# Picking experts on VectorE: masked copies over all heads at once, candidates' sums in two instructions, ranks in whole numbers

## The reference

```
v1, i1 = lax.top_k(s1, 16)          # (T, 8, 16); s2 likewise
v2, i2 = lax.top_k(s2, 16)
cand = (v1[..., :, None] + v2[..., None, :]).reshape(T, 8, 256)
sc, flat = lax.top_k(cand, 16)
e = take_along_axis(i1, flat // 16) * 128 + take_along_axis(i2, flat % 16)
g = softmax(sc)
out = sum over the 128 picks e of  g * gelu(x . u[e]) * v[e]
```

## Time and profile before

| | us |
|---|---|
| median of 3 runs | 1686.26 (1685.68 to 1686.49) |
| the profiled execution | 1687.21 |
| its span, first to last instruction | 1685.5 |
| TensorE busy in it | 1520.3 (90%) |
| VectorE busy | 1361.4 (81%) |
| GpSimd busy | 823.4 (49%) |
| ScalarE busy | 657.4 (39%) |
| mean granted TensorE clock | 0.951 of full |

### The profile page before, as it was taken

How to read it: one execution, slowest core, us unless ns; L and a number is a source line. 1 busy time by engine, 2 the same in 40 slices (tenths; PEclk the granted TensorE clock), 3 DMA queues, 4 the chain that set the end, 5 groups by cost and what they waited for, 6 DMA issues and landing times.

```text
span 1685.5 us, 25524 instructions
## 1 busy us (share of the span) xinstructions
PE 1520.3 (90%) x7943; PEld 1303.4 (77%) x7943; DVE 1361.4 (81%) x2701; ACT 657.4 (39%) x1101; POOL 823.4 (49%) x800
## 2 busy tenths in 40 slices
PE   4999799997978656768999999999999999999996
PEld 3677566684747545567999999999999999999995
DVE  5776544352579999848999999999999999999998
ACT  3332245421137663333443433434334334344343
POOL 1000100001029876637666676666666666766662
PEclk7999899998989857989999999999999999999998
DMA  9974121232000007899999999999999999999992
GB/s 348 357 267 159 64 73 50 100 129 74 1 1 1 1 13 227 256 299 407 406 403 385 382 382 388 383 379 392 383 379 387 388 379 384 386 383 384 384 387 103
DMA packets 193019, 448.90 MB, mean 266 GB/s; under 512 B 30699, under 2 KB 80131, under 8 KB 192716
## 3 DMA queue, kind: packets, MB, share of 16 engines
q1 hardware_dynamic: 136780, 243.65, 40.7%
q0 software_dynamic: 56192, 204.66, 31.0%
HBM read 424.57 MB, written 23.10 MB: 266 GB/s over the span
## 4 chain that ended last, share of the span: by engine, by line
PE 76%; DVE 12%; DMA 5%; issue 3%; POOL 2%; ACT 2%; SPq 1%; POOLq 0%; DVEq 0%; ACTq 0%
PE bank L818 13%; PE bank L993 9%; PE bank L992 9%; PE bank L991 9%; PE bank L1014 7%; PE bank L1012 7%; PE bank L1013 7%; PE bank L757 4%; PE bank L1004 3%; PE bank L1005 3%; PE bank L918 2%; DMA w_scratch<-staged 2%; DMA u_raw<-u_by_key 1%; DMA ring<-w_in 1%; POOL hot L692 1%
## 5 line engine op out<-in xcount | busy, mean ns | idle before, releaser
L991 PE MATMUL bank<-h_hi,u_hi 128*128 128x320 f32 x1024 | 316.5, 309 | 11.8 <-DVE u_lo L1807 11.8
L992 PE MATMUL bank<-h_lo,u_hi 128*128 128x320 f32 x1024 | 316.9, 310 | 0.0
L993 PE MATMUL bank<-h_hi,u_lo 128*128 128x320 f32 x1024 | 316.9, 309 | 0.0
L668 POOL DMA_INDIRECT v_rows<-v_exp,small x192 | 261.6, 1363 | 91.5 <-POOL small L664 51.8
L668 POOL DMA_INDIRECT u_rows<-u_exp,small x192 | 241.6, 1258 | 92.5 <-POOL small L664 51.2
L1323 ACT ACTIVATE v_hi<-v_raw 128x1024 fp32r<-128x1024 f32 x128 | 135.8, 1061 | 241.6 <-PE bank L1014 126.4
L991 PEld LDWEIGHTS bank<-h_hi,u_hi 128*128 128x128 f32 x1024 | 192.8, 188 | 17.2 <-issue 12.0
L1014 PE MATMUL bank<-v_hi,g_both 128*128 128x512 f32 x512 | 204.5, 399 | 0.0
L1012 PE MATMUL bank<-v_hi,g_both 128*128 128x512 f32 x512 | 203.6, 398 | 0.0
L1013 PE MATMUL bank<-v_lo,g_both 128*128 128x512 f32 x512 | 203.4, 397 | 0.0
L1807 DVE TENSOR_TENSOR u_lo<-u_raw,u_hi 128x1024 fp32r<-128x1024 f32 x128 | 157.4, 1231 | 55.2 <-ACT u_hi L1316 55.2
(11 more groups left out here) (247 smaller groups left out, 2940.4 us busy)
## 6 DMA issues: line engine op xcount, KB each, us to landing
u_raw<-u_by_key SPq DMA_DIRECT2D x128, 512.0 KB
v_raw<-v_exp SPq DMA_DIRECT2D x128, 512.0 KB
ada_blk<-ada_w SPq DMA_DIRECT2D x24, 1024.0 KB, 10.7
w_row<-w_scratch SPq DMA_DIRECT2D x128, 160.0 KB
ring<-w_in SPq DMA_DIRECT2D x18, 1024.0 KB, 5.1
w_scratch<-staged SPq DMA_DIRECT2D x2, 8192.0 KB, 30.8
xr<-x SPq DMA_DIRECT2D x8, 512.0 KB, 6.1
ring<-w_branch SPq DMA_DIRECT2D x4, 1024.0 KB, 5.1
```

What stands on the lines that cost most here:

```text
L668: pool.indirect_dma_start(out=rows[:, s], out_offset=None, in_=table, in_offset=bass.IndirectOffsetOnAxis(ap=ix[:, s:s + 1], axis=0))\
L991: pe.matmul(o, u_hi[:, r, k], h2_hi[:, k], start=(k == 0), stop=False)
L992: pe.matmul(o, u_hi[:, r, k], h2_lo[:, k], start=False, stop=False)
L993: last = pe.matmul(o, u_lo[:, r, k], h2_hi[:, k], start=False, stop=(k == KD - 1))
```

## The change

Four things change, all on VectorE:

- The masked copies of width 4, 2 and 1 run once over both halves of the heads instead of once per half. For that the lookup's scratch `halves` holds both halves; it lies in other places, one for tile 0, one for the tiles 1 and 2 (in two pieces 20 KB apart), one for tile 3. The piece of the tiles 1 and 2 takes the place of h2 of tile 1, so a wait for its transposes is added before pick(1).
- The sums of candidates are two instructions with four-dimensional patterns, all heads in each.
- The ranks stay whole numbers: the casts to float32 and back (L1689, L1704) go, and the instructions between read and write whole numbers.
- The two copies to `picks` stand together at the end.

```diff
--- before.py
+++ after.py
@@ -261,7 +261,15 @@
         top_i = at("top_i", 172, [P, 2 * PH, TOPK], U32)
         best = at("best", 173, [P, PH, TOPK])
         shifted = at("shifted", 173.5, [P, 2, P])
-        halves = at("halves", 28, [P, PH, TOPK, TOPK // 2])
+        halves_span = [at(f"halves{n}", kb, [P, kbs * 256]) for n, (kb, kbs) in enumerate(((35.5, 8), (167.5, 24), (135.5, 8)))]
+
+        def halves_of(t):
+
+
+            span = halves_span[(0, 1, 1, 2)[t]]
+            apart = 20 * 256 if t in (1, 2) else 1024
+            row = span.ap[0][0]
+            return bass.AP(span.tensor, 0, [[row, P], [apart, 2], [8, P], [1, 8]])
         starts = at("starts", 102.5, [P, P])
         expd = [at(f"expd{e}", kb, [P, P]) for e, kb in enumerate((91.5, 103, 108.5, 109))]
         h2 = [at(f"h2_{t}", kb, [P, D]) for t, kb in enumerate((183.5, 187.5, 183.5))] + [h2_own]
@@ -271,16 +279,14 @@
         def places_of(t):
 
             m = early if t == 0 else late
-            return (m[:, 0:384].bitcast(U32).rearrange("p (n h k) -> p n h k", n=3, h=PH),
-                    m[:, 384:768].rearrange("p (n h k) -> p n (h k)", n=3, h=PH),
-                    m[:, 768:1024].rearrange("p (h a k) -> p a h k", h=PH, a=2),
-                    m[:, 1024:1280].rearrange("p (n k) -> p n k", n=2 * PH))
+            return m[:, 0:384].bitcast(U32).rearrange("p (n h k) -> p n h k", n=3, h=PH), \
+                m[:, 1024:1280].rearrange("p (n k) -> p n k", n=2 * PH)
 
         def digits_of(t):
 
             m = early if t == 0 else late
             words = m[:, 0:1024].bitcast(U32).rearrange("p (n k) -> p n k", n=4)
-            return m[:, 768:1024], words[:, 0], (words[:, 1], words[:, 2], words[:, 3], words[:, 0])
+            return words[:, 3], (words[:, 1], words[:, 2], words[:, 0], words[:, 3])
 
         iota_f = small[:, 224:240]
         esum, einv = small[:, 240:248], small[:, 248:256]
@@ -1629,7 +1635,7 @@
 
                 stored(dve, *[("sc", t, q) for q in range(4)])
                 side = [scores[:, t % 2, n // 2, (n % 2) * NK:(n % 2 + 1) * NK] for n in range(2 * PH)]
-                place, place_n, pair, top_f = places_of(t)
+                place, top_f = places_of(t)
 
                 for n in range(2 * PH):
                     ins = dve.max(top[:, n, 0:8], side[n])
@@ -1646,12 +1652,12 @@
                 settled()
                 for i0, i1, nj in ((0, CORNER, TOPK), (CORNER, TOPK, CORNER)):
                     lo, n = (0, CORNER * TOPK) if i0 == 0 else (CORNER * TOPK, CANDS - CORNER * TOPK)
-                    shape = [P, i1 - i0, nj]
-                    for h in range(PH):
-                        ins = dve.tensor_tensor(
-                            cands[:, h, lo:lo + n].rearrange("p (i j) -> p i j", j=nj),
-                            top[:, 2 * h, i0:i1].unsqueeze(2).to_broadcast(shape),
-                            top[:, 2 * h + 1, 0:nj].unsqueeze(1).to_broadcast(shape), ALU.add)
+                    shape = [P, PH, i1 - i0, nj]
+                    by_side = top.rearrange("p (h a) k -> p h a k", a=2)
+                    ins = dve.tensor_tensor(
+                        cands[:, :, lo:lo + n].rearrange("p h (i j) -> p h i j", j=nj),
+                        by_side[:, :, 0, i0:i1].unsqueeze(3).to_broadcast(shape),
+                        by_side[:, :, 1, 0:nj].unsqueeze(2).to_broadcast(shape), ALU.add)
                 tick(ins)
                 for n in range(2 * PH):
                     ins = dve.max_index(top_i[:, n, 8:16], top[:, n, 8:16], side[n])
@@ -1686,49 +1692,43 @@
                     ins = dve.tensor_single_scalar(place[:, n], place[:, 0], by, ALU.logical_shift_right)
                 tick(ins)
                 settled()
-                tick(dve.tensor_copy(place_n, place))
-                settled()
-                i_of, j_of = pair[:, 0], pair[:, 1]
-                by_head = [place_n[:, n].rearrange("p (h k) -> p h k", h=PH) for n in range(3)]
+                as_number, ones_of = digits_of(t)
+                i_of, j_of = (as_number.rearrange("p (h a k) -> p h a k", h=PH, a=2)[:, :, a] for a in range(2))
                 first = starts.rearrange("p (h k) -> p h k", h=PH)
-                tick(dve.scalar_tensor_tensor(i_of, by_head[2], -float(TOPK - CORNER), by_head[1], ALU.add, ALU.max))
+                tick(dve.scalar_tensor_tensor(i_of, place[:, 2], -float(TOPK - CORNER), place[:, 1], ALU.add, ALU.max))
                 settled()
                 tick(dve.tensor_scalar(first, i_of, float(CORNER), float(CORNER * (TOPK - CORNER)),
                                        ALU.mult, ALU.add))
                 settled()
                 tick(dve.scalar_tensor_tensor(first, i_of, float(TOPK), first, ALU.mult, ALU.min))
                 settled()
-                tick(dve.tensor_tensor(j_of, by_head[0], first, ALU.subtract))
-                settled()
-                as_float, as_number, ones_of = digits_of(t)
-                tick(dve.tensor_copy(as_number, as_float))
+                tick(dve.tensor_tensor(j_of, place[:, 0], first, ALU.subtract))
                 settled()
                 for n in range(4):
                     tick(dve.tensor_scalar(ones_of[n], as_number, 3 - n, 1, ALU.logical_shift_right, ALU.bitwise_and))
                 settled()
 
 
+                wide, halves = [P, PH, TOPK, TOPK // 2], halves_of(t)
                 for half in range(2):
-                    sides, rows = slice(PH * half, PH * half + PH), slice(4 * TOPK * half, 4 * TOPK * half + 4 * TOPK)
-                    wide = [P, PH, TOPK, TOPK // 2]
-
-                    def where(n, width):
-                        at_half = ones_of[n][:, 2 * 4 * TOPK * half:2 * 4 * TOPK * (half + 1)]
-                        return at_half.rearrange("p (n k) -> p n k", n=PH).unsqueeze(3)\
-                            .to_broadcast([P, PH, TOPK, width])
-
-                    tick(dve.tensor_copy(halves, top_f[:, sides, 0:TOPK // 2].unsqueeze(2).to_broadcast(wide)))
+                    sides = slice(PH * half, PH * half + PH)
+                    at_half = ones_of[0][:, 2 * 4 * TOPK * half:2 * 4 * TOPK * (half + 1)]
+                    to = halves[:, half].rearrange("p (n k) j -> p n k j", n=PH)
+                    tick(dve.tensor_copy(to, top_f[:, sides, 0:TOPK // 2].unsqueeze(2).to_broadcast(wide)))
                     settled()
-                    tick(dve.copy_predicated(halves, where(0, TOPK // 2),
+                    tick(dve.copy_predicated(to, at_half.rearrange("p (n k) -> p n k", n=PH).unsqueeze(3).to_broadcast(wide),
                                              top_f[:, sides, TOPK // 2:TOPK].unsqueeze(2).to_broadcast(wide)))
+                settled()
+                for n, width in ((1, 4), (2, 2), (3, 1)):
+                    where = ones_of[n].rearrange("p (a k) -> p a k", a=2).unsqueeze(3).to_broadcast([P, 2, P, width])
+                    tick(dve.copy_predicated(halves[:, :, :, 0:width], where, halves[:, :, :, width:2 * width]))
                     settled()
-                    for n, width in ((1, 4), (2, 2), (3, 1)):
-                        tick(dve.copy_predicated(halves[:, :, :, 0:width], where(n, width),
-                                                 halves[:, :, :, width:2 * width]))
-                        settled()
-                    tick(dve.tensor_copy(picks[t][:, 0:2, rows].rearrange("p a (h k) -> p a h k", h=4),
-                                         halves[:, :, :, 0].rearrange("p (h a) k -> p a h k", a=2)))
-                    settled()
+                for half in range(2):
+                    rows = slice(4 * TOPK * half, 4 * TOPK * half + 4 * TOPK)
+                    ins = dve.tensor_copy(picks[t][:, 0:2, rows].rearrange("p a (h k) -> p a h k", h=4),
+                                          halves[:, half, :, 0].rearrange("p (h a k) -> p a h k", h=4, a=2))
+                tick(ins)
+                settled()
 
 
             def divide(t):
@@ -1756,6 +1756,7 @@
             multiplied(dve, ("h2T", 0, 0), ("h2T", 0, 1))
             h2_step(2)
             h2_step(3)
+            multiplied(dve, ("h2T", 1, 0), ("h2T", 1, 1))
             pick(1)
             pick(2)
             divide(1)
```

## The result

The changed kernel took 1688.47 us (median of 15 runs, 1686.61 to 1691.16), the kernel before 1686.17 (15 runs, 1684.08 to 1687.5): a ratio of 1.0017, with an interval of 1.0009 to 1.0024. It is 2.3 us slower. I had forecast 1684.9, and 1681.3 to 1687.2. The profiled execution took 1689.51 us with a span of 1687.8, 2.3 more than before.

A forecast was written before the change was run, and what follows sets the result against it. VectorE's picks were taken to bound the start of L1769, with GpSimd's line 5.2 us behind as cover. VectorE saves 7.5, GpSimd loses 3.8: 5.2 - 3.8 = 1.4 us gained, 1684.9 us; range 1681.3 to 1687.2.

The forecast's parts named there:

- What bounds the kernel: Before L1769 (`h_lo`): VectorE's picks end last; GpSimd's hot rows, staging and `h_hi` are late by 5.2 us less.
- Sums: Sums of candidates (L1651) on VectorE: 2.2 us become 1.15, saving 1.0 per pick.
- Casts: Casts in VectorE's ranks (L1689, L1704): removing two saves 0.8 us per pick; whole numbers cost nothing.
- Masked copies: VectorE's lookups (L1726): 1.28 us per merged copy; 0.5 saved per pick, plus 0.2 from less waiting and overlap.
- The added wait: Wait on h2(1)'s transposes before pick(1): already over when met, so costed at nothing.
- the second line: GpSimd's tile 0 hot rows, TensorE, ScalarE's staging and `h_hi`: delayed 3.8 us by VectorE's copies, between 2.2 and 6.3.
- `h_hi` follows GpSimd one for one: TensorE, the staging and ScalarE's `h_hi` move as much as GpSimd, so `h_hi` ends near 635.2.
- The rival "slower": GpSimd's groups under lookups of picks 1 to 3: loss 6.3 us, 1.1 slower, 1687.4; chance 0.08.
- point of decision: The kernel gets slower once a lookup costs GpSimd 4.0 us in each pick, against 2.9 now.
- +5.0: Estimated GpSimd delay by the skill's full blocking rule: 0.64 instead of 0.5 us for each of nine long copies.
- the row of 0.88: Profile row: a GpSimd instruction beginning under a masked copy of the 0.7 form takes 0.88 us.

The follow-up runs named there:

- e5: Kernel before with ScalarE's `h_hi` moved from behind all 32 groups to behind group 29: 1686.04 us, ratio 0.9997.
- e6: Kernel before, GpSimd writing zeros for tile 0's hot rows (its gates left out): 1683.3 us, ratio 0.9979 to before.
- e7: Changed kernel, GpSimd writing zeros for tile 0's hot rows (its gates left out): 1674.7 us, ratio 0.9932 to before.
- e1: Changed kernel with masked copies by half and `halves` in its old place again, new sums and ranks kept: 1683.83 us, ratio 0.9987 to before.
- e10: Changed kernel with both the edits of e1 and e4, copies by half and early `h_hi`: 1680.55 us, ratio 0.9974 to before.
- e4: Changed kernel with ScalarE's `h_hi` behind its group 29 instead of behind all 32: 1687.59 us, ratio 1.0008 to before.
- e12: e4 with VectorE's `h_lo` held until GpSimd's 32 groups are done: 1683.96 us, ratio 0.999 to the kernel before.

## Why the prediction was wrong

The mechanism was right in its main parts, and one term was too small; with it the sign of the sum turned.

- **What bounds the kernel.** Right. Two lines meet at `h_lo` with 5.2 us between them; e5, e6 and e7 show which was late in each kernel.
- **Sums: 1.0 saved.** Right: 1.16 for the two against 2.21.
- **Casts: 0.8 saved, whole numbers at nothing.** Right: the rank steps take 0.26 to 0.36 each.
- **Masked copies: 1.28 for 256 runs.** Right undisturbed, 1.25; merging and the wait less save 0.9 per pick there, 0.7 forecast. Beside GpSimd they take 1.27 to 1.38 (groups by shape of after, 482 to 640):

```profile
L1724 DVE COPY_PREDICATED halves<-lists,halves 128x512 f32<-128x512 uint32 x3 | 4.1, 1375 | 0.1
L1724 DVE COPY_PREDICATED halves<-lists,halves 128x1024 f32<-128x1024 uint32 x3 | 3.9, 1306 | 0.1
L1724 DVE COPY_PREDICATED halves<-lists,halves 128x256 f32<-128x256 uint32 x3 | 3.8, 1269 | 0.1
```

- **The added wait at nothing, `halves`' new places at nothing.** Right for the wait: none stands before pick(1). For the places nothing speaks against it, but no run changes them alone. Pick(2) does wait 1.81 us for scores, since the last of these is stored 2.8 us later than in the earlier trace rows (542.8 instead of 540.0); that used slack only, as I had said.
- **What happens to the second line: +3.8 us.** This is the step that failed. Measured +7.3, where my own upper bound was 6.3. Its parts: picks 1 and 2, forecast 1.2 less 0.2 for sums and casts, measured 1.3 + 1.7 = 3.0; pick(3), forecast 2.9 less 0.1, measured 4.3. In pick(3) the collision by itself was sized well: e1, with short copies, loses 3.5 there, 2.9 more than before. All the rest is the length of the copies, 15.5 - 11.3 = 4.2 us over three picks, 1.4 each. I had worked out 1.5 - 0.2 = 1.3 per pick, and then taken 0.6, as if gaps between the groups hid a part: for three picks that alone is 2.4 us too little, of the 3.5 that the sum missed (the rest lies in pick(3), where I had taken 0.3 off for its last copies, and in the sums and casts). The gaps hid nothing: the small copy in such a gap takes 0.65 or 0.46 itself, instead of 0.19. Nor did sums and casts give anything back: e1 loses 0.1 and 0.2 more than before beside picks 1 and 2.
- **`h_hi` follows GpSimd one for one.** Right, 6.8 and 6.8 (the loss of 7.3 less the 0.5 by which the first group began earlier). With the loss as measured the prediction's own sum gives 5.2 - 7.3 = 2.1 us slower; measured 2.3.

The rival "slower" named this place, and its point of decision: 4.0 us per lookup. The lookups cost GpSimd 4.5, 3.9 and 4.8 (the two slow groups and what lies between them), 13.2 in sum. I gave it 0.08. What spoke for it stood in the prediction: the rule of the Trainium skill, "SBUF — State Buffer", section Who interferes with whom, that a VectorE instruction with two SBUF inputs shuts out a GpSimd instruction that reads SBUF for its whole length. Its +5.0 was nearer to the 7.3 than my 3.8. The traces agree with it in part. Beside the long copies GpSimd's instructions end 0.2 to 1.2 us behind the copy under which they begin, as after a wait for its end. But they then run on under the next copy: in e1 that makes them nearly free, 0.79 to 0.88 us, so the row of 0.88 was typical of short copies and no outlier. It said nothing of copies of 1.28. For these the prediction had its own figure, 1.3 per pick, and halved it.

## What to carry to other kernels

When an engine on the path gets faster, work out what its instructions do to the line with the next least slack before counting the gain: here 7.5 us saved on VectorE cost GpSimd 7.3, and there were 5.2 between them. Two short VectorE instructions beside a busy GpSimd can be better than one long one, although the long one takes less time by itself (masked copies, e1 against after). Give the second line room first (an instruction moved out of a queue that it needn't stand in: e10), check that what starts earlier doesn't fall on the instruction that now ends last (e4 against e12), and follow the order behind the moved instruction to its next wait (divide(3) in e4).

## What the runs showed of the hardware

- A masked copy in runs of up to 4 elements costs by its runs and hardly by its elements: 128 runs of 4, 2 or 1 take 705 to 708 ns, 256 such runs 1249 to 1254. With runs of 8 the elements count: 128 of these take 1308 to 1314.
- How long one GpSimd instruction can be held. Its line 698 in after, 616 to 633 us, and the same line in e1 (ns, min/median/max):

```profile
L698 POOL TENSOR_SCALAR first_hot<-lane,small x14: 786/884/2361, 615.6 to 632.4; 128x128 f32<-128x128 f32 x14
```

```profile
L699 POOL TENSOR_SCALAR first_hot<-lane,small x12: 788/852/1848, 615.9 to 628.7; 128x128 f32<-128x128 f32 x12
```

  It is 2.36 us with the long copies, 1.85 with the short ones, 0.79 undisturbed. Its own 0.79 and one whole copy of 1.3 would be 2.1, so in the longest case it was held by more than one VectorE instruction in a row.
- The blocking goes both ways: the masked copies are up to 0.12 us longer beside GpSimd than alone, and before gains 3.3 us when GpSimd only writes zeros (e6).
